# The products of a mixture of experts put in a staggered order on TensorE

## The reference

```python
aff = softmax(h @ w_router)                       # 1024 tokens x 16 experts
g, idx = top_k(aff.T, 128)                        # each expert chooses 128 tokens
xin = h[idx]                                      # rows of expert x: 128 x 1024
a, u = xin @ w_gate[x], xin @ w_up[x]             # 1024 x 1024 weights each
y = (silu(a) * u) @ w_down[x] * g                 # for every one of 16 experts
out = x + g2 * scatter_add(y, idx)
```

## Time and profile before

| | us |
|---|---|
| median of 3 runs (2939.79, 2959.73, 2965.72) | 2959.73 |
| profiled execution, its own time | 2942.95 |
| its span, first to last instruction | 2941.2 |
| mean granted TensorE clock | 0.937 |
| PE busy over the span | 2511.8 (85%) |
| DVE busy | 1858.0 (63%) |
| ACT busy | 1201.9 (41%) |
| expert stage: first gather issued | 2266.2 |
| first product, last x_y | 2281.5, 2930.4 |

### The profile page before, as it was taken

The page is one execution under the profiler, slowest core; times in us unless marked ns, Lnnn a source line. Parts: engine busy times, 40 slices in busy tenths (PEclk is TensorE's granted clock), DMA queues, the critical chain, the costliest instruction groups (busy, mean ns, idle before and its releaser), DMA issues. The chain is left out here.

```text
span 2941.2 us, 31753 instructions
## 1 busy us (share of the span) xinstructions
PE 2511.8 (85%) x11533; PEld 1622.7 (55%) x11533; DVE 1858.0 (63%) x3258; ACT 1201.9 (41%) x1886; POOL 551.4 (19%) x531
## 2 busy tenths in 40 slices
PE   7999998899996999799999588679930899898987
PEld 3344443545556864465666377535420777676776
DVE  2799998687754213266554350556548788787886
ACT  2221111444543563354454331344320566565654
POOL 0000000021110000177676100001110122123221
PEclk9999999999998999999999799879965999999999
DMA  3014622011003320444432320021151889899895
GB/s 122 8 57 54 75 79 88 27 44 44 26 26 131 83 67 22 160 118 125 125 106 78 120 89 32 0 104 41 51 207 61 311 323 350 313 349 344 308 346 190
DMA packets 126264, 382.56 MB, mean 130 GB/s; under 512 B 22952, under 2 KB 31864, under 8 KB 124576
## 3 DMA queue, kind: packets, MB, share of 16 engines
q1 hardware_dynamic: 107360, 316.54, 30.2%
q0 software_dynamic: 18752, 64.00, 9.3%
HBM read 331.20 MB, written 49.31 MB: 129 GB/s over the span
## 5 line engine op out<-in xcount | busy, mean ns | idle before, releaser
L477 PE MATMUL ps<-l_hT,l_w 128*128 128x512 f32 (+1 forms) x832 | 363.9, 596 | 2.6 <-DVE l_hT L289 2.6
L477 PEld LDWEIGHTS ps<-l_hT,l_w 128*128 128x128 f32 (+1 forms) x832 | 155.3, 189 | 203.9 <-issue 203.7
L884 ACT ACTIVATE a_pT<-ps 128x512 f32<-128x512 f32 (+3 forms) x368 | 164.1, 486 | 171.5 <-PE ps L775 170.5
L2369 POOL DMA_INDIRECT out_dram<-x_y,e_token x16 | 93.0, 5814 | 507.4 <-DVE x_y L2494 507.4
L819 PE MATMUL ps<-l_wo,a_mixT 128*128 128x512 f32 x384 | 182.2, 602 | 2.1 <-ACT l_klT L908 0.9
L1263 DVE MAX8 l_best<-sel 128x8 f32<-128x384 f32 (+5 forms) x192 | 171.5, 893 | 5.4
L1264 DVE MATCH_REPLACE8 sel<-l_best,sel 128x384 f32<-128x384 f32 (+5 forms) x192 | 168.0, 875 | 0.0
L896 ACT ACTIVATE a_p<-ps,a_stat 128x384 f32<-128x384 f32 (+7 forms) x192 | 129.0, 672 | 92.1 <-DVE a_stat L958 53.3
L896 ACT ACTIVATE l_lat<-ps,a_stat 128x1024 f32<-128x1024 f32 (+7 forms) x128 | 94.8, 740 | 169.8 <-DVE a_stat L958 169.1
L760 PE MATMUL ps<-l_kT,l_raw 96*128 96x512 f32 (+3 forms) x384 | 147.2, 492 | 15.7 <-DMA l_raw<-qT_d 14.7
L2223 DVE TENSOR_TENSOR x_w1l<-x_raw,x_w1h 128x4096 fp32r<-128x4096 f32 x32 | 141.5, 4421 | 17.1 <-ACT x_w1h L2215 17.1
(11 more groups left out here) (361 smaller groups left out, 5594.5 us busy)
## 6 DMA issues: line engine op xcount, KB each, us to landing
x_raw<-in_w_gate SPq DMA_DIRECT2D x32, 2048.0 KB, 14.1
x_raw<-in_w_up SPq DMA_DIRECT2D x32, 2048.0 KB, 14.1
x_raw<-in_w_down SPq DMA_DIRECT2D x32, 2048.0 KB, 8.2
ada_w<-in_w_ada POOLq DMA_DIRECT2D x64, 384.0 KB, 3.7
l_w<-in_e_w_in SPq DMA_DIRECT2D x7, 2048.0 KB, 8.5
qT_d<-l_qT SPq DMA_DIRECT2D x8, 768.0 KB, 4.3
l_raw<-qT_d SPq DMA_DIRECT2D x8, 768.0 KB, 8.6
l_bias<-in_x SPq DMA_DIRECT2D x8, 512.0 KB, 3.7
```

The source lines that it names most:

```text
L477: last = nc.tensor.matmul(self.t.ps[0:m, bank, :], w[:, c, col * P:col * P + m], hT[:, c, half * 512:(half + 1) * 512], start=c == 0, stop ...
L884: self.k.nc.scalar.activation(dst, src, ACT.Copy).then_inc(self.moved["act"], 1)
L2369: nc.gpsimd.indirect_dma_start(t.out, bass.IndirectOffsetOnAxis(ap=token[:, x:x + 1], axis=0), yo[:], None, compute_op=ALU.add).then_inc(s ...
```

## The change

The list of TensorE becomes: gate(0); then for each x: up(x), gate(x+1) with the turns of h(x) ahead of its fourth chunk, down(x) with the turns of the rows of x+2 between its halves. The halves of weights are numbered in that new order (`at`), and SP loads them so. xT gets a second buffer pair. ScalarE in place of VectorE scales and shifts the turned rows, with eight activations of 128x128 from PSUM (`rows_x`). POOL's list is gather(x+2), scatter(x). Weight parts get new places on ScalarE and VectorE. The gain is loaded ahead of g2, and gets a semaphore of its own. The instructions of the products themselves are the same. Cut to its core:

```diff
-    def load(self, e, n, x=None):
-        i = n % 6
-        m, half = self.mats[i // 2], slice((i % 2) * self.HK * P, (i % 2 + 1) * self.HK * P)
-        src = m[n // 6, half, :] if x is None else m[bass.ds(x, 1), half, :].rearrange("a b c -> (a b) c")
+    def at(self, x, m):
+        if m == self.UP:
+            return 6 * x + 2
+        if m == self.GATE:
+            return 6 * x - 2 if x else 0
+        return 6 * x + 6 if x + 1 < EXPERTS else 6 * x + 4
+    def load(self, e, n, m, x):
+        half = slice((n % 2) * self.HK * P, (n % 2 + 1) * self.HK * P)
+        src = self.mats[m][x, half, :] if isinstance(x, int) else self.mats[m][bass.ds(x, 1), half, :].rearrange("a b c -> (a b) c")
         e.dma_start(self.raw[n % self.RAWS][:], rows(src)).then_inc(self.w_in[n % self.RAWS], 16)
+    def load_at(self, e, n):
+        for x in range(EXPERTS):
+            for m in range(3):
+                if self.at(x, m) == n // 2 * 2:
+                    self.load(e, n, m, x)
...
-        xT = [k.sb(f"x_T{part}", [P, KD, P], F32R) for part in "hl"]
+        xT = [[k.sb(f"x_T{i}{part}", [P, KD, P], F32R) for part in "hl"] for i in range(2)]
...
-            RAWS = weights.RAWS
             for n in range(SLOTS, 12):
                 if n >= RAWS:
                     e.wait_ge(w_split, n - RAWS + 1)
-                weights.load(e, n)
-            with e.Fori(1, EXPERTS // 2) as pair:
+                weights.load_at(e, n)
+            with e.Fori(1, EXPERTS // 2 - 1) as pair:
                 for n in range(12):
+                    m = (DOWN, UP, GATE)[n // 2 % 3]
                     e.wait_ge(w_split, pair * 12 + (n - RAWS + 1))
-                    weights.load(e, n, pair * 2 + n // 6)
+                    weights.load(e, n, m, pair * 2 + (n // 6 + {DOWN: -1, UP: 0, GATE: 1}[m]))
+            for n in range(weights.N - 12, weights.N):
+                e.wait_ge(w_split, n - RAWS + 1)
+                weights.load_at(e, n)
...
+                if x < EXPERTS:
+                    if x:
+                        e.wait_ge(xturn, 2 * x)
+                    nc.gpsimd.indirect_dma_start(xg[:], None, t.xn_d, bass.IndirectOffsetOnAxis(ap=token[:, x:x + 1], axis=0)).then_inc(gathered, 16)
             gather(0)
+            gather(1)
             for x in range(EXPERTS):
-                if x + 1 < EXPERTS:
-                    e.wait_ge(xturn, 2 * (x + 1))
-                    gather(x + 1)
+                gather(x + 2)
...
-            turn_x(0)
-            for x in range(EXPERTS):
-                e.wait_ge(xready, x + 1)
-                product(x, xT, 0, 0)
-                if x:
-                    e.wait_ge(hsplit, 2 * x)
-                product(x, xT, 1, 2)
-                if x + 1 < EXPERTS:
-                    turn_x(x + 1)
...
+            def turn_h(x):
                 e.wait_ge(hready, x + 1)
...
+            def gate(x, between=None):
+                e.wait_ge(xready, x + 1)
+                if x:
+                    e.wait_ge(silu, x)
+                for i in range(2):
+                    e.wait_ge(w_split, weights.at(x, GATE) + i + 1)
+                    for c in range(HK):
+                        if between is not None and i == 0 and c == HK - 1:
+                            turn_h(between)
+                        chunk(x, xT[x % 2], GATE, 0, i, c)
+            turn_x(0)
+            gate(0)
+            for x in range(EXPERTS):
+                if x:
+                    e.wait_ge(hsplit, 2 * x)
+                for i in range(2):
+                    e.wait_ge(w_split, weights.at(x, UP) + i + 1)
+                    for c in range(HK):
+                        chunk(x, xT[x % 2], UP, 2, i, c)
+                    if x == 0 and i == 0:
+                        turn_x(1)
+                if x < LAST:
+                    gate(x + 1, x)
+                else:
+                    turn_h(x)
                 if x:
                     e.wait_ge(yready, x)
+                for i in range(2):
+                    e.wait_ge(w_split, weights.at(x, DOWN) + i + 1)
+                    e.wait_ge(hsplit, 2 * x + i + 1)
+                    for c in range(HK):
+                        chunk(x, hT, DOWN, 6, i, c)
+                    if i == 0:
+                        turn_x(x + 2)
...
         @block.scalar
         def _(e):
-            def x_high(x):
-                e.wait_ge(xmoved, 2 * x + 2)
-                if x:
-                    e.wait_ge(w_used, 6 * x - 2)
-                nc.scalar.activation(flat(xT[0][:]), flat(xf[:]), ACT.Copy).then_inc(xhigh, 1)
-            x_high(0)
+            def rows_x(x):
+                if x < EXPERTS:
+                    if x:
+                        e.wait_ge(xready, x)
+                    for c in range(KD):
+                        e.wait_ge(xturn, 2 * x + c // 4 + 1)
+                        last = nc.scalar.activation(xf[:, c, :], ps[:, 4 + c // 4, (c % 4) * P:(c % 4 + 1) * P], ACT.Identity,
+                                                    scale=gain[:, c:c + 1], bias=t.mod[:, 3 * KD + c:3 * KD + c + 1])
+                    last.then_inc(xmoved, 1)
+                    e.wait_ge(xmoved, x + 1)
+                    if x >= 2:
+                        e.wait_ge(w_used, done(x - 2, UP))
+                    nc.scalar.activation(flat(xT[x % 2][0][:]), flat(xf[:]), ACT.Copy).then_inc(xhigh, 1)
+            def first_of_h(x):
+                if x < EXPERTS:
+                    e.wait_ge(w_used, done(x, GATE))
+                    if x:
+                        e.wait_ge(hturn, 2 * x)
+                    nc.scalar.activation(h[:], ps[:, 0:2, :].rearrange("p a n -> p (a n)"), ACT.Silu).then_inc(silu, 1)
+            e.wait_ge(gained, 1)
+            rows_x(0)
+            weights.high(e, 3)
+            weights.high(e, 4)
+            first_of_h(0)
             for x in range(EXPERTS):
-                weights.high(e, 6 * x + 3)
-                weights.high(e, 6 * x + 4)
-                e.wait_ge(w_used, 6 * x + 2)
-                if x:
-                    e.wait_ge(hturn, 2 * x)
-                nc.scalar.activation(h[:], ps[:, 0:2, :].rearrange("p a n -> p (a n)"), ACT.Silu).then_inc(silu, 1)
                 weights.high(e, 6 * x + 5)
+                if x == 0:
+                    rows_x(1)
+                weights.high(e, 6 * x + 6)
                 for i in range(2):
                     e.wait_ge(hturn, 2 * x + i + 1)
+                    if x:
+                        e.wait_ge(w_used, done(x - 1, DOWN))
                     nc.scalar.activation(flat(hT[0][:, 4 * i:4 * i + 4, :]), ps[:, 2 + i, :], ACT.Copy).then_inc(hhigh, 1)
-                weights.high(e, 6 * x + 6)
-                if x + 1 < EXPERTS:
-                    x_high(x + 1)
                 weights.high(e, 6 * x + 7)
                 weights.high(e, 6 * x + 8)
+                first_of_h(x + 1)
+                weights.high(e, 6 * x + 9)
+                rows_x(x + 2)
+                weights.high(e, 6 * x + 10)
         @block.vector
         def _(e):
-            link.eng = e
-            def move_x(x):
-                if x:
-                    e.wait_ge(xready, x)
-                for i in range(2):
-                    e.wait_ge(xturn, 2 * x + i + 1)
-                    dst = xf[:, 4 * i:4 * i + 4, :]
-                    col = lambda ap: ap[:, 4 * i:4 * i + 4].unsqueeze(2).broadcast_to([P, 4, P])
-                    link(nc.vector.tensor_tensor(dst, ps[:, 4 + i, :].rearrange("p (c n) -> p c n", n=P), col(gain), ALU.mult))
-                    nc.vector.tensor_tensor(dst, dst, col(t.mod[:, 3 * KD:4 * KD]), ALU.add).then_inc(xmoved, 1)
             def low_x(x):
-                e.wait_ge(xhigh, x + 1)
-                nc.vector.tensor_tensor(flat(xT[1][:]), flat(xf[:]), flat(xT[0][:]).bitcast(F32), ALU.subtract).then_inc(xready, 1)
+                if x < EXPERTS:
+                    e.wait_ge(xhigh, x + 1)
+                    nc.vector.tensor_tensor(flat(xT[x % 2][1][:]), flat(xf[:]), flat(xT[x % 2][0][:]).bitcast(F32),
+                                            ALU.subtract).then_inc(xready, 1)
             e.wait_ge(small, 32)
+            nc.vector.scalar_tensor_tensor(gain[:], t.mod[:, 4 * KD:5 * KD], 1.0, gain[:], ALU.add, ALU.mult).then_inc(gained, 1)
             weights.low(e, 0)
-            link(nc.vector.scalar_tensor_tensor(gain[:], t.mod[:, 4 * KD:5 * KD], 1.0, gain[:], ALU.add, ALU.mult))
-            move_x(0)
             low_x(0)
-            weights.low(e, 1)
-            weights.low(e, 2)
+            for n in range(1, 5):
+                weights.low(e, n)
             for x in range(EXPERTS):
-                weights.low(e, 6 * x + 3)
-                weights.low(e, 6 * x + 4)
+                weights.low(e, 6 * x + 5)
+                if x == 0:
+                    low_x(1)
                 e.wait_ge(silu, x + 1)
-                e.wait_ge(w_used, 6 * x + 4)
+                e.wait_ge(w_used, done(x, UP))
```

(66 more changed lines are left out.)

7 lines of the change are left out of this document (3 added, 4 removed).

## The result

The changed kernel takes 2870.86 us (median of four runs, 2867.40 to 2872.38), against 2954.14 for the kernel before (four runs, 2939.79 to 2965.72): a ratio of 0.9719, 95% interval 0.9671 to 0.9766. In a later call it was 2872.51 against 2939.87, 0.9745 (0.9700 to 0.9791). The profiled execution took 2871.80 us with a span of 2870.0, 71 us under the profiled one of before. Ratios leave out runs over 1.5% above the fastest of the same kernel: two, both of the kernel before in the first call of the experiments (2995.31 and 2998.47 us). Predicted were 2912, with 2880 to 2944 as the range: the direction was right, the size outside, since I had put the gain at 44 us.

A forecast was written before the change was run, and what follows sets the result against it. With transfers as the pace, 77.8 us plus 14 rounds of 37.6 gave 604.2 against 648.9 us, 44 less net. Taken from 2959.73 and 2952, that gave 2916 and 2908, predicted as 2912, range 2880 to 2944.

The forecast's parts named there:

- The transfers become the pace: Expert stage: moving 13.63 MB an expert at 363 GB/s takes 37.6 us a round, more than TensorE's 36.1.
- P: Length of each of 14 middle rounds of the expert stage, taken as 37.6 us, forecast range 37.0 to 38.4.
- the ends: Expert stage outside the 14 rounds: start 13.3, first round 38.4, last expert 26.1, in all 77.8 us.
- TensorE's own floor: Three products and 16 turns on TensorE without waits: 36.08 us a round.
- TensorE-paced rival: Transfers keep up, rounds of 36.1 to 36.8 us, 56 to 66 us less, about 2890; chance 0.25.
- The sum: Expert stage total: 77.8 + 14 rounds of 37.6 gives 604.2 us against 648.9, 44 us less net.
- The walk through one round: Step-by-step times of TensorE, ScalarE, VectorE and POOL in one round of 36.1 us; nearly each low part 4.3 us early.
- the tight place: h on VectorE, behind one low part, is ready 0.3 to 0.6 us before its turns on TensorE.
- The gathers: On POOL, gathers issued a round earlier land 8.4 us before wanted; late gathers and both long rounds go.
- The second rival: The new order is partly tied again at h: rounds of 38.6 to 39.5 us, 2930 to 2948; chance 0.22.
- The slower rival: Four raw weight buffers serving six loads set the pace: rounds of 42.0 us, 2977 in all; chance 0.09.

The follow-up runs named there:

- experiment 7: The kernel before, unchanged, profiled twice more: 2935.26 and 2953.18 us.
- Experiment 8: Changed kernel with weight parts moved behind the rows or h for expert 0 and behind h(T) for the last: 2862.69 us, later 2861.83 against 2872.51 unmended.
- experiment 6: Changed kernel with VectorE again scaling and shifting the turned rows in place of ScalarE: 2938.22 us, ratio 1.0012 to the kernel before.
- experiments 5: Changed kernel with the turns of h(x) behind gate(x+1), not ahead of its fourth chunk: 2919.98 us, ratio 0.9826 to the kernel before.
- experiment 2: Changed kernel without the matmuls on the low left part, weight parts from half 6 on a quarter wide: one run, 2838.89 us.

## Why the prediction was wrong

**The step that failed is "The transfers become the pace", P = 37.6 us.** Measured: 35.2 in the changed kernel, where TensorE is the pace, with a floor of the transfers of 34.35. Over 14 rounds that is 33.6 us. From gate(0) to the end of the last down the stage takes 576.9 us against my 604.2, so 27.3 less: the 33.6 less 6.3 by which the ends, below, were longer. The other 13 of the 41 us between 2912 and 2870.86 are the base. I worked out the 44 us from the profiled execution at 2943 and took them off about 2956, as if the changed kernel kept what made other executions slower. By the three traces of the kernel before (experiment 7) that is long scatters with gathers behind them; the change makes them harmless, and its four runs agree within 5 us.

I had divided 341 GB/s by the share of 0.94 and called 363 GB/s the full rate; per full share it is 397/1.03 = 386 with gathers and scatters, 409/1.03 = 397 for loads alone, and the share itself goes to 1.03. With 386 a round is 35.3 us, with 397 it is the measured 34.3. The share is time that packets took, and not work, and the rate per share is not one number. Two stretches of the kernel before with a low share (columns as in the earlier trace rows):

```profile
2567.50:2570.00 2.50, 0.93 (x4) 0.67 (x4) 2.50 (x3) 2.50 (x2) 0.00 (x0) 1.00 0.51 157
2607.50:2610.00 2.50, 1.35 (x6) 1.13 (x7) 2.50 (x2) 2.50 (x2) 0.00 (x0) 1.00 0.56 121
```
Scaled to a full share these are 308 and 216 GB/s, against 421 at 1.03. In both one load is ending and the next, issued at 2568.07 and at 2607.49, is beginning. Such stretches go into the mean, but they are only part of the error: in steps of 2.5 us from 2540 to 2690 all 60 give 361 GB/s per full share, the 46 with a share of 0.95 or more 372, and 386 is more than either. The rest, and why the rate per share falls, was not taken apart. The bound that I worked out from the best stretches, 34.1, was right within 0.3 us and should have led, but that is partly luck: its parts were 29.9 for the loads and 4.2 for gather and scatter, measured are 30.7 and 3.65. The 421 GB/s are not weights alone, as I had it. The queues from 2590.0 to 2592.5 (packets, MB, share):

```profile
q1 hardware_dynamic: 218, 0.84, 82.2%
q0 software_dynamic: 67, 0.21, 20.6%
```

By the Trainium skill (DMA: Bandwidth & Descriptors, Specifications) a core gets about 358 GB/s of HBM; my estimate from it was a round of 38.1 us. As a limit for this kernel that is refuted: 397 GB/s over 360 us. Another page of the Trainium skill (HBM Reference, Specifications (TRN2)) says when the first figure holds: with both cores of a pair streaming; a core alone measures about 425. This kernel runs on one core, and the 409 of loads alone is near that.

**TensorE's own floor, 36.08, was too high** by 0.89 us. The rate of 0.2353 held the first matmul of a run and its end, and I took eight turns at 1.09 from a stretch in which TensorE had just waited; in a stream they are 0.2323 and 0.87. So even the TensorE-paced rival, which has the right mechanism and had a chance of 0.25, gave 56 to 66 us where the traces show 71. It is 12.5 us over 14 rounds, inside the 33.6 above. No value of P that I held possible could give the measured one. (Between up and the next gate of the earlier trace rows lie 16.5 us, not 16.4; nothing hangs on it.)

**The ends, 77.8 us, were 84.1** (2282.30 to 2859.23 less 14 x 35.2). The start is 2.6 long: after the wait for the rows of x=1, which is 3.2 us in place of 2.3, 18 matmuls take 5.80 us in place of 4.2, with a granted clock of 0.76 from 2311 to 2317. At the end it is 3.7: ScalarE's high part 95 and VectorE's low part stand ahead of h (6.35 us between up and down, not 3.5), and the last down takes 13.13, behind that wait at 0.68 for 6 us. The sum had no term for the clock behind a wait, other than in gate(0). I had looked for what covers h in a round, and priced the last one from the kernel before, whose order of parts it no longer had. Experiment 8 mended both. These are the same two costs, a wait and the slower matmuls behind it, that made experiment 6 miss its 37.5 us.

**The walk through one round was right**, step by step, and it is what carries the gain. The high parts of the trace start behind TensorE's halves, 5.6 us apart but for the turns and for the one that stands behind the rows; x_h is ready at 2492.28 and wanted near 2492.7, the tight place that I named with 0.3 to 0.6 us of room; it never failed in 14 rounds. The eight activations take 2.88 us, the lower bound, not my 3.6. The estimate from the Trainium skill (ScalarE: Activation LUTs, What ACT_TABLE_LOAD costs), 3.1, lay nearer than mine. **The gathers** go as predicted: TensorE waits for none, and the cover holds also for late ones. **The second rival**, an order tied again with rounds of 38.6, did not come, but experiments 5 and 6 show how near it is: turns behind the gate give 38.0, rows on VectorE 39.25 to 39.65. **The slower rival**, the ring of raw buffers: landing has a median of 11.2 us, and between 2340 and 2820 neither ScalarE nor TensorE waited for a load; refuted.

**What each part is worth**, by round: late gathers gone, 40.7 to 39.1; with all of the change but the turns inside, 38.0; with all but the rows on ScalarE, 39.4; whole, 35.2. The parts don't add: in these orders the turns inside and the rows on ScalarE each give most of their gain only with the other. What remains is TensorE's own stream.

## What to carry to other kernels

A share of busy DMA time is no measure of what is left: take the rate from the best stretches with the same mix, and check it by a kernel in which nothing else can pace. Price an engine's floor from the middle of an unbroken stream, not from a run with its first and last instruction. Price a wait of TensorE with what follows it: here waits of 2.5 us or more were followed by up to 1.8 us of slower matmuls, in some rounds and not in others, and what decides it these runs do not say. And where engines keep written orders, walk through one round with them: a part fits if each step is in time, not if the busy times add up to less than the round; then walk through the first and the last round too. A gain worked out from one execution is taken off that execution, unless what makes the others slower stays.

## What the hardware showed that was not expected

The scatter of the kernel before has three lengths on POOL, and what sets them is VectorE. Alone it is 1.57 us. Started at 2574.98, inside a low part that ran from 2574.62 to 2579.04, it took 5.52 us and ended 1.46 after that low part. The long one started at 2489.63, with these beside it on VectorE:

```profile
2489.27 4.42 DVE L2223 TENSOR_TENSOR x_w2l<-x_raw,x_w2h 128x4096 fp32r<-128x4096 f32 x1
2493.60 4.42 DVE L2223 TENSOR_TENSOR x_w0l<-x_raw,x_w0h 128x4096 fp32r<-128x4096 f32 x1
2499.10 4.43 DVE L2223 TENSOR_TENSOR x_w1l<-x_raw,x_w1h 128x4096 fp32r<-128x4096 f32 x1 [1.07 <-ACT x_w1h L2215]
```
It ended at 2499.48, 1.46 us after the second of them. So by the times POOL waits until VectorE lets go, and where two such instructions follow each other it gets in between them or misses, which is a lottery of 4.33 us: 7 misses in 45 in the three traces of the kernel before, 16 in 30 in the two with the gather ahead. What decides it is open. In the changed kernel the same scatter has a median of 2.32 us: it starts beside the 1.2 us low part of xT and again ends 1.46 us after it; only the scatter of expert 14, beside a whole low part of a weight, takes 5.56. The Trainium skill (SBUF — State Buffer, SBUF: two separate sides) says that VectorE with two SBUF inputs and GpSimd lock each other out of a shared port pair for a whole instruction, against a GpSimd operation that reads SBUF; these rows agree for the issue of an indirect DMA. In experiment 2, where the weight parts are a quarter wide, VectorE is idle when most scatters start, and they take 1.59 to 1.60 us:

```profile
2458.35 1.59 POOL L2389 DMA_INDIRECT out_dram<-x_y,e_token  x1 [31.07 <-DVE x_y L2536]
```
```profile
2459.53 1.23 DVE L2508 TENSOR_TENSOR x_T0l<-x_f,x_T0h 128x1024 fp32r<-128x1024 f32 x1 [1.46 <-ACT x_T0h L2472]
```
That VectorE's instruction beside it sets the length is therefore shown; that a shared port is the reason is the account of the Trainium skill, and was not tested.
